# A hybrid RG-LRU / attention / mixture-of-experts step: the last two expert tiles returned to token order by TensorE instead of through DRAM

## The reference, cut to what matters

```python
w = take_along_axis(scores, idx, -1); w = w / sum(w)      # top 2 of 16 experts, within the best group
combine = sum(one_hot(idx, 16) * w[..., None], axis=1)
for e in range(16):
    a = silu(t @ w_exp_gate[e]) * (t @ w_exp_up[e])        # 1024 -> 512
    y = y + combine[:, e:e+1] * (a @ w_exp_down[e])        # 512 -> 1024
x = x + g2 * y                                             # g2: one vector for context, one for latent tokens
out = rms_norm(x, final_norm_g)
```

## Time and profile before

| what | value |
|---|---|
| median of 3 runs | 1199.46 us (1199.22 to 1202.29) |
| the profiled execution | 1198.25 us, with a span of 1196.3 us |
| PE busy | 1107.3 us, 93% of the span |
| DVE busy | 909.7 us, 76% |
| ACT busy | 678.9 us, 57% |
| POOL busy | 256.1 us, 21% |
| DMA moved | 232.17 MB, mean 194 GB/s |

### The profile page before, as it was taken

One profiled execution on the slowest core, in us unless ns is written; L12 is line 12 of the kernel. 1 busy time (PEld: TensorE's weight loads), 2 busy tenths in 40 slices (PEclk: granted clock), 3 DMA queues, 4 the chain that ended last, 5 costly groups with the idle time before them and its releaser, 6 DMA issues.

```text
span 1196.3 us, 19808 instructions
## 1 busy us (share of the span) xinstructions
PE 1107.3 (93%) x7082; PEld 1014.9 (85%) x7082; DVE 909.7 (76%) x1255; ACT 678.9 (57%) x1041; POOL 256.1 (21%) x139
## 2 busy tenths in 40 slices
PE   5999999999999999999999999995999999999950
PEld 1599999999999998899999999995788888888840
DVE  6748797978879796866556637558799998999928
ACT  3646757666666756642222212455688877877824
POOL 0132222122222122233333323201110110110011
PEclk9899999999999999999999999997999999999985
DMA  9235412212111221134444445538799999999945
GB/s 366 98 113 160 148 48 81 72 67 84 56 63 57 79 69 50 41 130 152 140 140 141 140 148 192 173 114 316 291 396 421 424 411 418 405 414 427 366 151 200
DMA packets 54569, 232.17 MB, mean 194 GB/s; under 512 B 5328, under 2 KB 22000, under 8 KB 46064
## 3 DMA queue, kind: packets, MB, share of 16 engines
q1 hardware_dynamic: 50480, 216.79, 48.2%
q0 software_dynamic: 4032, 14.68, 3.2%
HBM read 210.45 MB, written 21.00 MB: 193 GB/s over the span
## 4 chain that ended last, share of the span: by engine, by line
PE 50%; DVE 4%; ACT 1%; issue 1%; DMA 1%; POOL 0%; DVEq 0%; SPq 0%; ACTq 0%; POOLq 0%
PE PS L943 24%; PE PS L710 21%; PE PS L935 1%; PE PS L815 1%; PE PS L956 1%; PE PS L860 1%; DVE xo L1947 1%; DVE xo L1949 1%; DVE hrow L1780 0%; PE PS L906 0%; DMA G<-slot_rows,slotI 0%; DVE yo L1959 0%; DVE WgLo L1883 0%; DVE acc L1604 0%; PE PS L848 0%
## 5 line engine op out<-in xcount | busy, mean ns | idle before, releaser
L604 POOL TENSOR_TENSOR wLo<-wRaw,wHi 128x1024 fp32r<-128x1024 f32 x80 | 202.9, 2537 | 547.3 <-ACT wHi L1020 547.2
L710 PE MATMUL PS<-hHi,wHi 128*128 128x320 f32 x896 | 285.2, 318 | 4.3 <-DVE hLo L1435 1.9
L710 PE MATMUL PS<-hLo,wHi 128*128 128x320 f32 x896 | 277.4, 310 | 0.0
L710 PE MATMUL PS<-hHi,wLo 128*128 128x320 f32 x896 | 277.4, 310 | 0.0
L710 PEld LDWEIGHTS PS<-hHi,wHi 128*128 128x128 f32 x896 | 169.4, 189 | 5.6 <-issue 3.2
L710 PEld LDWEIGHTS PS<-hLo,wHi 128*128 128x128 f32 x896 | 169.1, 189 | 0.0
L710 PEld LDWEIGHTS PS<-hHi,wLo 128*128 128x128 f32 x896 | 168.8, 188 | 0.0
L1604 DVE SCALAR_TENSOR_TENSOR acc<-adaL,csil,acc 128x512 f32<-128x512 f32 x112 | 103.8, 985 | 10.3 <-DMA adaL<-in_w_ada_late 9.9
L1020 ACT ACTIVATE wHi<-wRaw 128x1024 fp32r<-128x1024 f32 x80 | 84.1, 1051 | 44.8 <-PE PS L710 44.7
L1883 DVE TENSOR_TENSOR WgLo<-Wg,WgHi 128x2048 fp32r<-128x2048 f32 x34 | 76.4, 2287 | 13.0 <-ACT WgHi L1241 12.9
L1883 DVE TENSOR_TENSOR WdLo<-Wd,WdHi 128x2048 fp32r<-128x2048 f32 x34 | 76.4, 2288 | 9.5 <-ACT WdHi L1241 9.2
(11 more groups left out here) (324 smaller groups left out, 2764.9 us busy)
## 6 DMA issues: line engine op xcount, KB each, us to landing
wRaw<-in_wtiles SPq DMA_DIRECT2D x80, 512.0 KB, 3.4
Wu<-in_experts SPq DMA_DIRECT2D x18, 2048.0 KB, 9.4
Wg<-in_experts SPq DMA_DIRECT2D x18, 2048.0 KB, 9.7
Wd<-in_experts SPq DMA_DIRECT2D x17, 2048.0 KB
adaL<-in_w_ada_late SPq DMA_DIRECT2D x32, 512.0 KB, 4.3
slot_rows<-Ys SPq DMA_DIRECT2D x18, 512.0 KB, 10.7
ada<-in_w_ada SPq DMA_DIRECT2D x8, 1024.0 KB, 17.7
slot_rows<-tab SPq DMA_DIRECT2D x10, 512.0 KB, 6.5
```

The costliest lines, as they stand in the source:

```text
L604: nc.gpsimd.tensor_tensor(wLo[b][:], wRaw[b][:], wHi[b][:].bitcast(F32), ALU.subtract).then_inc(w_lo, 1)
L710: r = mm(PS[:, bank, 0:HALF], w[:, k, :], x[:, k, cols], start=(k == 0 and w is wHi[b] and x is xh), stop=(k == KT - 1 and w is wLo[b]))
```

## The change

- Only tiles 0 to 15 of 18 (all but the last two) go through `slot_rows`. ACT multiplies each row by its weight while it copies the tile out of PSUM, with a weight by slot, `wslot`. That list is made by PE like `idxI`, from three fp16 parts of the weight: ten matmuls 78 columns wide, which PE does before `h_cols` of tile 0. Slots in the last two tiles point to a row of zeros instead.
- DVE's new small steps stand in two places: seven of them ahead of the first `weights_low(1, 0)`, and nine (`slot_weights`) between it and the first `h_low(0, 0)`. The write of `slotI` moves from the first part into the last.
- POOL gathers, at the time tiles 16 and 17 are transposed, the g2 row of each slot's token (`G2s`). The ten gathers of result rows start once the rows of tile 15 are stored; the first five are plain, the other five add to the same buffer in the DMA (`compute_op=ALU.add`), each after the plain one of its token tile.
- The last two tiles are multiplied in PSUM by weight and g2 (DVE, `yg`), split in a high (ACT) and a low part (DVE), and multiplied by PE with one-hot matrices `mark`, 128 slots to 128 tokens. The residual is added in the same PSUM bank by a full fp32 matmul of the identity with `x1t`. DVE multiplies the five gathered tiles with g2 (`gated`) and adds PSUM to each (`summed`); `xo` and `yo` have five buffers.
- `g2b` is loaded earlier, `final_g` later; the first half of the last down weights' low part moves ahead of `aS`. SP fills twelve tiles and one row with zeros instead of ten tiles.

The diff, cut to its core:

```diff
 # SP
-                        for t in range(E, NT):
+                        for t in range(E - 2, NT):
                             sp.dma_start(yd[t * P:(t + 1) * P, :]..., tab[...]).then_inc(zero_row, 16)
+                        sp.dma_start(yd[NT * P:NT * P + 1, :]..., tab[0:1, ...]).then_inc(zero_row, 16)
...
         rows_out(2 * more + (E - 3), 1)
+        sp.wait_ge(u_mm, 2 * more + (E - 1))
+        for g in range(2):
+            sp.dma_start(g2b[g][:]..., g2d...broadcast_to([P, KT, P])).then_inc(gb_in, 16)
         sp.wait_ge(W_lo_ok[2], 2 * more + (E - 1))
+        sp.wait_ge(gg_ok, 1)
         sp.dma_start(fgb[:], final_g.broadcast_to([P, D])).then_inc(gb_in, 16)
-        rows_out(2 * more + (E - 2), 0)
-        rows_out(2 * more + (E - 1), 1)
 # POOL
+        for i in range(2):
+            pool.wait_ge(ht_mm, 2 * more + (E - 1 + i))
+            nc.gpsimd.indirect_dma_start(out=G2s[i][:], in_=g2d..., in_offset=...group2[:, i:i + 1]...)
+        pool.wait_ge(W_lo_ok[1], 2 * more + E)
+        pool.wait_ge(W_lo_ok[2], 2 * more + (E - 1))
         for b in range(2):
-            pool.wait_ge(ys_out[b], 16 * more + 8 * E)
+            pool.wait_ge(ys_out[b], 16 * more + 8 * (E - 2))
         for t in range(TT):
-            for x, G in enumerate((G1, G2)): ...
+            nc.gpsimd.indirect_dma_start(out=G[t][:], in_=yd, in_offset=...slotI[:, 0, t:t + 1]...)
+        for t in range(TT):
+            pool.wait_ge(gy_in[t], 16)
+            nc.gpsimd.indirect_dma_start(out=G[t][:], in_=yd, in_offset=...slotI[:, 1, t:t + 1]...,
+                                         compute_op=ALU.add).then_inc(gy_in[t], 16)
 # PE
+        pe.wait_ge(oh_ok, 3)
+        for n in range(2 * TT):
+            x = mm(PS[:, 5, 160:160 + 3 * NT], ohP[:, n, :], ohW[:, n]..., ...)
...
+        def residual(t, h):
+            if t >= 4:
+                pe.wait_ge(x2_ok, t - 3)
+            mm(PS[:, (2 * t + h) % 8, :], C("ident"), x1t[:, t, h * 512:(h + 1) * 512], start=True, stop=False)
+        def spread(t, h):
+            for i in range(2):
+                pe.wait_ge(yl_ok, 1 + i * (1 + h))
+                for y in (ygH, ygL):
+                    x = mm(PS[:, (2 * t + h) % 8, :], mark[i][:, tok(t)], y[i][:, h * 512:(h + 1) * 512], ...)
         a_cols(2 * more + (E - 1))
+        residual(0, 0); residual(0, 1)
-        down(2 * more + (E - 1), 0)
+        down(2 * more + (E - 1), True)      # waits yg_ok instead of ys_ev
+        residual(1, 0); residual(1, 1)
+        for h in range(2):
+            for t in range(2):
+                spread(t, h)
+        for t in range(2, TT):               # both halves: residual, then spread
 # ACT
-                A(Ys[1 - b][:]..., PS[:, 6:8, :], ACT.Copy).then_inc(ys_ev, 1)
+                A(Ys[1 - b][:]..., PS[:, 6:8, :], ACT.Copy, scale=wslot[:, bass.ds(t - 1, 1)]).then_inc(ys_ev, 1)
+        A(ygH[0][:], yg[0][:], ACT.Copy); two halves of ygH[1]; one ACT.Sqrt ahead of its use
+        for t in range(TT): Square with sum, Sqrt
 # DVE, in its order after the activation of the last tile
+        v.scalar_tensor_tensor(yg[0], PS[:, 6:8, :], ws2[:, 0:1], G2s[0], ALU.mult, ALU.mult)   # waits d_mm, hs_in[0]
         expert(2 * more + E, 0, last=True, rows_only=True)                                      # aTL
+        slot_marks(2 * more + (E - 1))       # idx2, rel, mark[0], mark[1] (128 x 640 each)
+        out_low(0, 1, slice(0, D))
+        out_half(0); gated(0); out_low(1, 2, slice(0, 512))
+        out_half(1); gated(1); out_low(1, 3, slice(512, D))
+        for t in range(2, TT):
+            gated(t)                         # waits gy_in[t] >= 32; G[t] * g2b
+        summed(0)                            # waits oc_mm t+1; xo[t] = PSUM + G[t]
+        for t in range(1, TT):
+            summed(t); normed(t - 1)         # normed waits sqo_ok; reciprocal, xo * stat * fgb
+        normed(TT - 1)
```

More of the change, by code:

```diff
@@ L237, in build @@
     pb = region(gb_at)
-    g2b = pb("g2b", [2, D])
     fgb = pb("fgb", [D])
+    G4 = pb("G4", [D])
+    mark = [pb(f"mark{i}", [T], F32R) for i in range(2)]
+    assert pb.at[0] <= gb_at + 4 * KT * FE
+    g2b = [region(hS_at + 8 * D + 8 * KT * P * g)(f"g2b{g}", [D]) for g in range(2)]
+    G2s = [region(hS_at + 4 * D * i)(f"G2s{i}", [D]) for i in range(2)]
     p5 = region(p3.at[0])
@@ L957, in a_cols, with down @@
             x.then_inc(at_mm, 1)
-        def down(t, m=2):
+        def down(t, last=False):
+            m = 0 if last else 2
             pe.wait_ge(at_lo, t + 1)
             pe.wait_ge(W_lo_ok[2], t + 1)
-            wait(pe, ys_ev, t)
+            if last:
+                pe.wait_ge(yg_ok, 1)
+            else:
+                wait(pe, ys_ev, t)
             for h in range(2):
@@ L966, in down @@
                             slice(0, FE))
+                if last and h == 0:
+                    x.then_inc(d_mm, 1)
             x.then_inc(d_mm, 1)
@@ L1924, in _ @@
         weights_low(1, 0)
+        slot_weights()
         h_low(0, 0)
@@ new lines, in _, with gated, out_half @@
+        slot_marks(2 * more + (E - 1))
+        dve.wait_ge(gb_in, 64)
+        def gated(t):
+            dve.wait_ge(gy_in[t], 32)
+            v.tensor_tensor(G[t][:], G[t][:], g2b[min(t, 1)][:], ALU.mult).then_inc(gg_ok, 1)
+        def out_half(h):
+            cols = slice(h * 512, (h + 1) * 512)
+            dve.wait_ge(d_mm, 2 * more + (E + h))
+            v.scalar_tensor_tensor(yg[1][:, cols], PS[:, 6 + h, :], ws2[:, 1:2], G2s[1][:, cols], ALU.mult, ALU.mult) \
+                .then_inc(yg_ok, 1)
@@ new lines, in normed @@
+        def normed(t):
+            if t == 0:
+                dve.wait_ge(gb_in, 80)
+            dve.wait_ge(sqo_ok, t + 1)
+            st(v.reciprocal(stat[:, 10 + t:11 + t], stat[:, 5 + t:6 + t]))
+            seq.last()
+            v.scalar_tensor_tensor(yo[t][:], xo[t][:], stat[:, 10 + t:11 + t], fgb[:], ALU.mult, ALU.mult) \
+                .then_inc(out_ok, 1)
+        out_low(0, 1, slice(0, D))
+        dve.wait_ge(hs_in[1], 16 * more + 8 * E + 16)
+        out_half(0)
+        gated(0)
@@ L1962, in build @@
+        out_low(1, 2, slice(0, 512))
+        out_half(1)
+        gated(1)
+        out_low(1, 3, slice(512, D))
+        for t in range(2, TT):
+            gated(t)
+        summed(0)
+        for t in range(1, TT):
+            summed(t)
+            normed(t - 1)
+        normed(TT - 1)
     ctx.close()
```

240 lines of the change are left out of this document (160 added, 80 removed).

## The result

The changed kernel takes 1194.78 us (median of 7 runs, 1193.25 to 1198.38). The kernel before took 1201.91 on the same chip (7 runs). The ratio is 0.9938, 95% interval 0.9915 to 0.9960. So it is faster by 0.6%, clear of the interval and of the 0.3% that I had set for no change; but that is 7.1 us, where I had forecast 16.8, and the time lies outside my range.

The account below looks back on a forecast made before the run. The prediction took TensorE to bound the kernel, with a 42.0 us tail where it idles. Span 1196.3 - 18.3 (tail) + 1.3 (front) + 0.2 (zeros) = 1179.5, a median of 1182.7 us; range 1178 to 1192.

Parts of the forecast that it names:

- DVE wants it at 1159.3. The margin is 2.3 us.: Tail: the last gathered rows land at 1157, before DVE needs them, so the gathers stay hidden.
- the doubled price: Tail: each adding gather taken at twice a plain one, 2.6 us, so the last rows land at 1160.5.
- rival B: Tail: ten gather issues wait for DVE, up to 1.25 us more each; 1193 at worst, about 1187 if half; chance 0.06.
- I count 0: Tail: doubled adding gathers cost 1 us at most, inside the overlap of PE's pace, so nothing was added.
- rival A: Tail: adding gathers land late, last rows at 1167, then 18.3 us to the end; median 1190; chance 0.18.
- The 1157: Tail: landing time of the last gather, from adding issues ending at 1151.6 and 5.5 us to land.
- The front: Before the first expert: nine tiny slot_weights steps on DVE delay hSL, which PE awaits; 1.3 us, bounds 0 to 2.5.
- PE's half clock held longer by its wait: Front: part of the reason for its upper bound of 2.5 us, beside steps of 0.25 each.
- The zeros: SP's extra zero stores move the weight load from 124.16 to 127.7; 0.2 us, bounds 0 to 1.5.
- the cover of 0.8: Zeros: slack between the weight load's landing at 131.1 and ACT's start on it at 131.91.
- The bound on the gathers: Tail: range kept for adding gathers landing late, 0 to 8 us, with 0 counted in the sum.

Follow-up runs that it names:

- e9: e6 with the final gain's row (fgb) loaded as soon as both g2b rows have landed; 1188.06 us, ratio 0.9897 to the kernel before, tail 35.1 us.
- e6: Changed kernel, tile 17's halves and low parts before the first gated, sums and norms between gated tiles, slot_weights after hSL, ten zero stores; 1188.91 us, ratio 0.9914.
- e11: e9 with the second five gathers plain, overwriting rows instead of adding; 1181.47 us, ratio 0.9850 to the kernel before, tail 32.0 us.
- e7: Changed kernel with the last down weights' low part made for only 32 of 2048 columns of each half; 1184.79 us (one run), tail 37.1 us.
- e3: Changed kernel with slot_weights put back behind the first h_low and ten zero stores instead of twelve; 1193.27 us, ratio 0.9926 to the kernel before.

## Why the prediction was wrong

The direction was right, the last two tiles did go through TensorE at the price forecast, and PE's and DVE's part of the sum held. The step that was to hide the gathers behind that work did not, nor did two terms of the front. On the profiled executions the forecast span was 1179.5 and the measured one is 1192.9, 13.4 more.

1. **"DVE wants it at 1159.3. The margin is 2.3 us."** This is the step that failed, worth 8.8 us of tail (40.8 against 32.0). Counted from the transposes, DVE wanted the last rows at +13.3. They were to land at +11.0 (1157), or at +14.5 (1160.5) by the doubled price that I said I took, which already was past the mark; they landed at +22.9. The chain of that number:
   - The first issue came at -6.0 instead of -6.8: the stored rows landed in 8.4 us, against 7.8. Small.
   - *Issues held by DVE* cost 3.6 us on the first two. I had rival B for it, with a chance of 0.06, because few of the gather issues of the expert stage are longer than 0.96. That row didn't show what I took from it: there the small copy just ahead of each issue had mostly waited out DVE's instruction already (up to 2.0 us), and the new gathers have no such copy. A price was read from a place where another instruction paid it. The trace of before had the right row, which I overlooked: the gather of the second tile has no copy ahead of it, and its issue took 2.67 us, again to 0.81 us behind the end of a low part (the first half of WuLo, from 822.69 on the earlier trace rows).

```profile
823.12 2.67 POOL L634 DMA_INDIRECT hS<-h_rows,idxI  x1 [0.30 <-issue]
```

   - The first adding gather landed 7.0 us after its issue and the others about 2.5 us apart. The doubled DMA price (2.6) was right. What was wrong was to write "I count 0" behind it.
   - The load of `fgb`, issued at 1164.20 behind the first gated tile, coincides with the last two gaps between landings, 3.9 and 3.1 instead of 2.5; in e9, where it goes out 17 us earlier against the transposes, all are 2.5. I had no term for it, though the diff shows the wait. e6 and e9 differ in this load alone: from the first adding landing to the fifth they take 11.3 and 9.9 us, so the load costs 1.3 there. The changed kernel's 12.2 leaves 0.9 more, which stays open.
   - I checked only the last gather against DVE. The first was wanted at +6.3 and came at +10.8. DVE runs in order, so that wait held PE as well, and the ten sums and norms stood behind all four waits: the 17.9 us behind the last landing that rival A had worked out. What happened is rival A with B's late start.
   - The 1157 was also misread by 1.2 us to the safe side: I counted the 5.5 from the end of the last issue, and the view counts a landing from the issue's start. That gives 1155.9 and a margin of 3.4, and would not have saved the step.
2. **The front, 1.3 us.** It costs 2.4. The steps are 1.2, about as forecast; the other 1.2 is what "PE's half clock held longer by its wait" stood for, which I had only as a bound (2.5).
3. **The zeros, 0.2 us.** They cost 1.0 in this trace: SP's twelve stores and the single row took 22.1 us instead of some 19, so the cover of 0.8 was gone.
4. **What is left**, 13.4 - 8.8 - 1.1 - 0.8 = 2.7: 2.3 of it had come up before `idxI` (821.23 before, 824.55 after, less 1.0 for the zeros), where the two executions have their clock stretches at different places, and a stall at 357 that only after's has. I don't count it to the change; that the medians are 7.1 us apart and the profiled spans 3.4 points the same way, but no run shows it.

Right were: the last `down` (ended near +7.9, forecast +7.9), 3.57 us a tile on PE, the fp32 matmuls at 0.43 a record, DVE's instructions, the scale on Ys (1.12 us, no PE wait from it), and PE's clock, which stayed up but for a stretch behind its 2.43 us wait (0.53 from 1164.5 to 1168), where DVE was the chain anyway. That the last stretch cost nothing follows from DVE's waits and was not tried. The bound on the gathers ("0 to 8") did not hold: they cost 8.8. The chance that I gave to the cases in which they are late, 0.18 + 0.06, was too small for a margin of 2.3 us under three unpriced terms.

## What to carry to other kernels

Where an in-order engine has several waits for a DMA, check the first of them and not only the last, and list what stands behind each: here a late first tile held the other engine, and ten independent steps stood behind the last one. Putting both right, together with the early `fgb`, took 5.7 us off the tail (e9), where making the gathers plain as well took only 3.1 more (e11). When you take a price from a row, look at the instruction just ahead of it; it may have paid a wait that your new place will pay itself. Interleave the finishing steps with the arrivals, and look for small loads whose issue was tied to an event that the new order makes late.

## What the runs showed of the hardware

- An adding gather of 512 KB took twice the DMA time of a plain one: landings 2.5 us apart (e9) against 1.3 (e11, the second five), with the DMA engines full both times and moving 211 and 397 GB/s. Where DVE didn't hold it, its issue took 1.54 to 1.58 us on POOL and that of a plain one 0.94.
- A gather's issue, which reads its indices, ended 0.81 us behind the end of DVE's running two-input instruction, and took up to 3.0 us in all; when that instruction was cut short (e7) the five plain ones took 0.93 to 0.94 each.
- 1.0 us more idle of PE ahead of the first product (3.5 instead of 2.5) went with twelve of its first matmuls at 1.2 GHz, instead of six or seven, in seven profiles of seven; that is 1.2 us on top. With the shorter idle one profile of six (e3) had the twelve too.
